# A hybrid decoder layer with 32 experts on one core: experts in 14 tiles instead of 16, a last tile by columns, two banks for head outputs, other places for S5 and the first loads

## The reference

```python
xn = rms_norm(h, mix_norm_g[l])
proj = jnp.einsum('bsd,de->bse', xn, w_in[l])
q_a, k_a, v_a, u_s5, q_h, f_h, i_h, g_h = jnp.split(proj, split_at, axis=-1)
attn_out = diff_attention(...)     # 6 heads, two softmaxes per head
s5_out = s5_mixer(...)             # 40 groups, 64 states, then z * sigmoid(z @ w_glu)
hgrn_out = hgrn2_mixer(...)        # 5 heads
mix = jnp.concatenate([attn_out, s5_out, hgrn_out], axis=-1)
h = h + jnp.einsum('bse,ed->bsd', mix, w_out[l]).astype(h.dtype)
hn = rms_norm(h, ffn_norm_g[l])
h = h + hier_moe(hn, ...)
return rms_norm(h, final_norm_g)
```

```python
expert_id = (g_idx[:, None] * EXPERTS_PER_GROUP + top_idx).reshape(-1)
order = jnp.argsort(expert_id)
xs = xt[order // TOP_K_IN_GROUP]
sizes = jnp.bincount(expert_id, length=N_EXPERTS).astype(jnp.int32)
h = jax.nn.silu(lax.ragged_dot(xs, w_gate, sizes)) * lax.ragged_dot(xs, w_up, sizes)
y = lax.ragged_dot(h, w_down, sizes) * gates_flat[order][:, None]
out = jnp.zeros_like(xt).at[order // TOP_K_IN_GROUP].add(y)
```

## Time and profile before

| | |
|---|---|
| median of 3 runs | 2043.24 us (2040.47 to 2047.9) |
| the profiled execution | 2040.63 us, its span 2038.7 us |
| mean granted clock of TensorE | 0.972 of full speed |
| busy: TensorE products / weight loads | 93% / 58% |
| VectorE / ScalarE / GpSimd | 40% / 12% / 9% |
| moved by DMA | 507.8 MB, 249 GB/s over the span |

### The profile page before, as it was taken

How to read it: one execution, slowest core, us unless ns; L and a number is a source line. 1 busy time by engine, 2 the same in 40 slices (tenths; PEclk the granted TensorE clock), 3 DMA queues, 4 the chain that set the end, 5 groups by cost and what they waited for, 6 DMA issues and landing times.

```text
span 2038.7 us, 32619 instructions
## 1 busy us (share of the span) xinstructions
PE 1899.3 (93%) x13695; PEld 1176.1 (58%) x13695; DVE 817.7 (40%) x1544; ACT 249.8 (12%) x551; POOL 189.5 (9%) x218
## 2 busy tenths in 40 slices
PE   5999999999999979999399998999999989999996
PEld 3888999789987869999233333332333323333332
DVE  6666585177456644333412121221222222122215
ACT  3012111100334331000200000000000000000002
POOL 1353332000000000000110000000000000000000
PEclk9999999999998989999699999999999999999998
DMA  5243333211221232121799999999999999999992
GB/s 210 85 146 92 90 97 85 94 63 42 71 74 58 68 141 82 65 82 42 304 422 424 423 425 422 408 424 416 411 423 404 423 412 410 423 403 423 391 378 104
DMA packets 74276, 507.81 MB, mean 249 GB/s; under 512 B 19184, under 2 KB 19332, under 8 KB 38160
## 3 DMA queue, kind: packets, MB, share of 16 engines
q1 hardware_dynamic: 56576, 485.60, 59.2%
q0 software_dynamic: 5728, 15.81, 2.3%
q10 hardware_dynamic: 11824, 4.17, 1.1%
HBM read 503.53 MB, written 12.99 MB: 253 GB/s over the span
## 4 chain that ended last, share of the span: by engine, by line
PE 80%; DMA 10%; DVE 4%; issue 3%; ACT 2%; SPq 0%; DVEq 0%; POOL 0%; POOLq 0%; ACTq 0%
PE psum L1151 21%; PE psum L850 19%; PE psum L853 15%; PE psum L1113 10%; DMA arena<-in_moe_w_gate 9%; PE psum L1170 7%; DVE arena L1453 2%; PE psum L1006 2%; PE psum L907 1%; PE psum L1126 1%; DMA arena<-hs_rows,arena 1%; DVE arena L1456 1%; PE psum L995 0%; DVE arena L2092 0%; PE psum L967 0%
## 5 line engine op out<-in xcount | busy, mean ns | idle before, releaser
L1151 PE MATMUL psum<-arena 128*32 128x512 f32 x4096 | 471.0, 607 | 37.9 <-issue 29.8
L1453 DVE TENSOR_TENSOR arena<-psum,arena 128x512 f32<-128x512 f32 x359 | 240.5, 687 | 443.4 <-PE psum L1113 423.9
L850 PE MATMUL psum<-arena 128*128 128x128 f32 x3584 | 412.9, 277 | 2.6 <-issue 2.6
L850 PEld LDWEIGHTS psum<-arena 128*128 128x128 f32 x3584 | 407.8, 194 | 9.8 <-issue 9.3
L1151 PEld LDWEIGHTS psum<-arena 128*32 128x32 f32 x4096 | 133.3, 112 | 367.3 <-issue 366.1
L853 PE MATMUL psum<-arena 128*128 128x256 f32 x1456 | 324.8, 382 | 1.9 <-DVE arena L533 1.3
L853 PEld LDWEIGHTS psum<-arena 128*128 128x128 f32 x1456 | 274.9, 191 | 40.8 <-issue 3.8
L1453 DVE TENSOR_TENSOR arena<-arena,psum 128x256 f32<-128x256 f32 (+2 forms) x174 | 76.5, 440 | 439.1 <-PE psum L850 211.3
L1113 PE MATMUL psum<-arena 128*128 128x512 f32 x512 | 236.0, 605 | 0.9 <-issue 0.9
L1170 PE MATMUL psum<-arena 128*32 128x512 f32 x2048 | 225.0, 597 | 2.6 <-DMA arena<-in_moe_w_down 2.1
L1453 DVE TENSOR_TENSOR arena<-arena 128x128 f32<-128x128 f32 (+17 forms) x446 | 177.8, 440 | 38.3 <-ACT arena L1230 30.1
(11 more groups left out here) (194 smaller groups left out, 950.1 us busy)
## 6 DMA issues: line engine op xcount, KB each, us to landing
arena<-in_moe_w_gate SPq DMA_DIRECT2D x64, 2048.0 KB, 23.9
arena<-in_moe_w_up SPq DMA_DIRECT2D x64, 2048.0 KB, 22.7
arena<-in_moe_w_down SPq DMA_DIRECT2D x64, 2048.0 KB, 22.7
arena<-in_w_in SPq DMA_DIRECT2D x86, 512.0 KB, 4.7
arena<-in_w_out SPq DMA_DIRECT2D x32, 512.0 KB, 4.6
arena<-in_x SPq DMA_DIRECT2D x8, 1024.0 KB, 8.8
hs_rows<-arena SPq DMA_DIRECT2D x4, 1024.0 KB, 5.1
out<-arena SPq DMA_DIRECT2D x4, 1024.0 KB, 4.0
```

Of the source, the lines that this page charges most:

```text
L850: last = mm(B(bank, [(1, P)], off=t * P), F(a + t * P, P), F(w + i * P, P), start=start and t == 0, stop=(i == KH - 1), skip_group_check=True)
L1151: last = mm(B(bank, [(1, FE)], 32 * g, 32), F(XT + c * CAP + 32 * g, 32), F(SLOT[slot] + (c % 8) * FE, FE), start=(c == 0), stop=(c == KD ...
L1453: return v.tensor_tensor(o, a, b, op)
```

## The change

1. **Tiles.** The 32 experts go into 14 tiles. `OWNERS` says which expert a group of 32 rows belongs to, `RANKS` which ranks (by size) a tile holds: the first tile has four experts with 32 rows each (ranks 16 to 19), eight tiles have 96 + 32 rows (rank i with rank 31 - i), four have 64 + 64 (8 + i with 15 - i), and the last again has four (20 to 23). TensorE's loop covers the eight; the four and both ends are written out. A table from the host gives each rank its rows; seven small operations of VectorE on the ranks go, two come ahead of `order_ready`.
2. **Loads.** SyncE reads four expert numbers and issues 24 halves for the first tile, then the loop of six iterations, then the last tile: 16 halves of gate and up, and its down weights by columns (four loads of columns 0 to 1023, four of 1024 to 1535, four of 1536 to 2047 that share the slots of the second four).
3. **Last tile.** The tile before it is combined as a whole first. TensorE spreads the final gain from one row over the partitions by four products. The down product and the combine go by quarters of 512 columns: quarters 0 and 1, their combines, quarter 2, its combine, quarter 3, its combine. Squares are summed by quarter on ScalarE, the gain is multiplied in by quarter on VectorE, and the scaling is shared: blocks 0 and 2 on VectorE, 1 and 3 on ScalarE.
4. **Attention's banks.** `ao` alternates between banks 3 and 2; the small steps have banks 0 and 1 plus spare ones. `attn_out` stands one unit later.
5. **S5.** For the last of the five blocks, `y5`, `yt` and `ge` stand at 9, 11 and 14 gaps instead of 10, 14 and 17.
6. **Start.** ScalarE takes a square root ahead of x. VectorE makes the first two weight sums ahead of the discretization; the sum `S4` of x (two operations) moves from the others to behind the first product, and TensorE waits for it at the seventh.
7. The overflow block gets semaphores of its own and is not overlapped with the tiles.

```diff
+CMIN = 32
+THREE_ONE, TWO_TWO, FOUR = (0, 0, 0, 1), (0, 0, 1, 1), (0, 1, 2, 3)
+OWNERS = [FOUR] + [THREE_ONE] * 8 + [TWO_TWO] * 4 + [FOUR]
+RANKS = [(16, 17, 18, 19)] + [(i, 31 - i) for i in range(8)] + [(8 + i, 15 - i) for i in range(4)] + [(20, 21, 22, 23)]
+NTILE = len(OWNERS)
+LAST = NTILE - 1
+A_END, B_END = 9, 13
...
+            y_at, yt_at, ge_at = (10, 14, 17) if more_ else (9, 11, 14)
...
-                          (6, [("sc", b, 4)]), (7, [("sc", b, 5)]), (10, [("y5", b, 0), ("y5", b, 1)]),
+                          (6, [("sc", b, 4)]), (7, [("sc", b, 5)]), (y_at, [("y5", b, 0), ("y5", b, 1)]),
...
             elif s[0] == "al":
-                small, ticking = [0, 1, 2], True
+                small, ticking = [0, 1], True
...
+            elif s[0] == "w4":
+                spare = [5, 6, 7]
             elif s[0] == "pe":
-                spare = []
+                spare = ([5, 6, 7], [6, 7], [], [])[s[1]]
...
-                bank = 3
+                bank = 3 - s[1] % 2
...
-            with sp.Fori(0, NPAIR // 2) as it:
+            four, parts = [expert(k) for k in range(4)], first_parts()
+            for j in range(FOUR_L):
+                part(four[j % 4], parts[j], j // 8, j // 4 % 2)
+            with sp.Fori(1, 1 + (B_END - 1) // 2) as it:
+                    two_, parts = [expert(it * 4 + 2 * k + i) for i in range(2)], pair_parts(it, k)
+                    for j in range(PAIR_L):
+                        part(two_[j % 2], parts[j], j // 4, j // 2 % 2)
...
+            sp.wait_ge(xT_full, 4 * B_END)
+            sp.dma_start(F(FG, D, 0, 1), DV(d["final_norm_g"], 0, [(D, 1), (1, D)])).then_inc(fg_in, 16)
+            four, parts = [expert(NE - 4 + k) for k in range(4)], last_parts()
+            for j in range(16):
+                part(four[j % 4], parts[j], j // 8, j // 4 % 2)
...
+            for k in range(4):
+                slot, n = parts[20 + k]
+                sp.wait_ge(slot_used[slot], n + 1)
+                sp.dma_start(V(SLOT[slot], [(512, FT2), (1, 512)]),
+                             down_columns(four[k], D // 2, 512)).then_inc(slot_in[slot], 16)
+            for k in range(4):
+                slot = parts[20 + k][0]
+                sp.dma_start(V(SLOT[slot] + D, [(512, FT2), (1, 512)]),
+                             down_columns(four[k], D // 2 + 512, 512)).then_inc(tail_in, 16)
             for t in range(TB):
-                sp.wait_ge(out_ready, t + 1)
+                sp.wait_ge((out_dve, out_act)[t % 2], 2 * (t // 2 + 1))
                 sp.dma_start(DV(out, t * P * D, [(D, P), (1, D)]), F(H0 + t * D, D)).then_inc(out_done, 16)
...
                     elif p == 0 and n == 2:
                         once(xsum_ready, 2)
+                    elif p == 0 and n == 6:
...
+                def y_part(q):
+                    here = parts[16 + 4 * (q // 2):20 + 4 * (q // 2)]
+                    if q == 3:
+                        pe.wait_ge(tail_in, 4 * 16)
+                    elif q != 1:
+                        for slot, before in here:
+                    for m in range(FT2):
+                        for g in range(4):
+                            at_ = m * (D // 2) + q * 512 if q < 2 else (q - 2) * D + m * 512
+                            last = mm(B(4 + q, [(1, 512)], 32 * g, 32), F(HTE + m * CAP + 32 * g, 32),
+                                      F(SLOT[here[g][0]] + at_, 512), start=(m == 0), stop=(m == FT2 - 1))
+                    last.then_inc(y_full, 1)
...
+                def combine_part(q):
+                    pe.wait_ge(y_act if q % 2 == 0 else y_dve, 2 * n + 2 + q // 2)
+                    if q == 0:
+                    for t in range(TB):
+                        if q:
+                            pe.wait_ge(comb_done, 16 * n + 4 * (q - 1) + t + 2)
+                        mm(B(t, [(1, 512)]), F(SEL + t * P, P), F(YSB + q * 512, 512), start=True,
+                           stop=True).then_inc(comb_full, 1)
+
+                y_part(0)
+                y_part(1)
+                combine_part(0)
+                combine_part(1)
+                y_part(2)
+                combine_part(2)
+                y_part(3)
+                combine_part(3)
...
-            for k in range(2):
-                pair_tile(k, k, 0, [pair_part(0, k, j) for j in range(12)], k > 0)
-            with pe.Fori(1, NPAIR // 2) as it:
+            expert_tile(0, 0, 0, first_parts(), FOUR, False)
+            with pe.Fori(1, 1 + (A_END - 1) // 2) as it:
                 for k in range(2):
-                    pair_tile(it * 2 + k, k, it, [pair_part(it, k, j) for j in range(12)])
+                    expert_tile(it * 2 - 1 + k, 1 - k, it - 1 + k, pair_parts(it, k), THREE_ONE)
+            for n in range(A_END, B_END):
+                expert_tile(n, n % 2, n // 2, pair_parts((n + 1) // 2, (n + 1) % 2), TWO_TWO, True, n + 1 < B_END)
...
+                pe.wait_ge(comb_done, 16 * LAST + 1)
+                with pe.Fori(0, NOV) as it:
+                    over_tile(it)
+                pe.wait_ge(o_added, NOV * 16 + 1)
+            turn(LAST, LAST % 2, LAST // 2, (0, 1, 2, 3), False, 16 * LAST)
+            pe.wait_ge(xT_free, 4 * LAST + 4)
+            last_tile(LAST, last_parts())
...
             act.wait_ge(eps_set, 1)
+            A(F(SM, 1), F(EPSC, 1), ACT.Sqrt)
             for t in range(TB):
...
+            y_copy(LAST, 2)
             for t in range(TB):
-                act.wait_ge(comb_done, 16 * (NPAIR - 1) + 4 * t + 5)
-                if t == 0:
-                    act.wait_ge(fg_in, 16)
-                deviation([F(H0 + t * D, D)], F(SLOT[7], D), SSQ + t, STD + t, D).then_inc(sum_std, 1)
+                square(t, 2)
...
+            def scaled(t):
+                act.wait_ge(h_rst, t + 2)
+                act.wait_ge(g_done, t // 2 + 1)
+                h = H0 + t * D
+                A(F(h, 1536), F(h, 1536), ACT.Copy, scale=F(RST + t, 1)).then_inc(out_act, 1)
+                A(F(h + 1536, 512), F(HG3 + t * 512, 512), ACT.Copy, scale=F(RST + t, 1)).then_inc(out_act, 1)
...
-                settle(tt(half(S2), half(S1), half(A11), SU))
-                last = tt(half(S4), half(A12), half(S2), SU)
+                last = tt(half(S2), half(S1), half(A11), SU)
...
+                        weight_sum(dve, v, 0, 0)
+                        weight_sum(dve, v, 0, 1)
                         disc_a()
                         disc_b()
...
+                elif s == ("pj", "u", 0):
+                    dve.wait_ge(xsum_ready, 1)
+                    tt(F(S4, KH * HB), F(A12, KH * HB), F(S2, KH * HB), SU).then_inc(xsum_ready, 1)
...
-                    if u >= 6 and u % TB == 2:
+                    if u > TB and u % TB == TB - 1:
                         attn_out(u // TB - 1)
...
+            dve.wait_ge(ranks_ready, 1)
+            two32 = [(NE, 2), (1, NE)]
+            settle(tt(V(ROP, two32, 0, NE), V(ROH, [(0, 2), (1, NE)], 0, NE), V(PLACE, two32, 0, NE), M))
+            settle(v.tensor_reduce(F(RMY, 2, 0, NE), V(ROP, two32, 0, NE), AX.X, AD))
...
+            for q in range(2):
+                for t in range(TB):
+                    add(t, q)
+            for q in range(2):
+                for t in range(TB):
+                    times_g(t, q)
...
+                add(t, 2)
+            for t in range(TB):
+                times_g(t, 2)
+            y_copy(3)
...
+            def scaled(t):
+                h = H0 + t * D
+                ts(F(h, 1536), F(h, 1536), F(RST + t, 1), None, M).then_inc(out_dve, 1)
+                v.scalar_tensor_tensor(F(h + 1536, 512), F(h + 1536, 512), F(RST + t, 1), F(FG + 1536, 512), M,
+                                       M).then_inc(out_dve, 1)
...
+            add(0, 3)
+            add(1, 3)
+            sum_of(0)
+            last_g(1)
+            add(2, 3)
+            inverse_of(0)
+            sum_of(1)
+            add(3, 3)
+            inverse_of(1)
+            scaled(0)
+            sum_of(2)
+            last_g(3)
+            inverse_of(2)
+            sum_of(3)
+            inverse_of(3)
+            scaled(2)
```

404 lines of the change are left out of this document (272 added, 132 removed).

## The result

| | before | changed |
|---|---|---|
| median of 4 runs | 2043.0 us | 1990.7 us (1987.7 to 1994.2) |
| ratio, 95% interval | | 0.9742 (0.9717 to 0.9766) |
| profiled execution, span | 2038.7 us | 1989.3 us |
| first weight load issued | 991.35 | 968.97 |
| last weight load landed | 1984 (a trickle until 1985.5) | 1962.9 |

The kernel is 2.6% faster. The forecast was 1985, inside a range of 1968 to 2008. Of the 49.4 us of the span, 22.4 come ahead of the first load and 28.3 behind the last landing; between the two they take the same within what can be told (993.9 for 992.7 up to 1984, or 994.2 up to 1985.5: in the old kernel the last packets of the weights trickle on at a DMA share of 0.08). The 28.3 and the 22.4 are the whole gain.

A forecast was written before the change was run, and what follows sets the result against it. TensorE was taken to bound the kernel up to 991 us, weight transfers after. First load at 968 plus 988 gave a last landing at 1956, plus 25 a span of 1981; forecast median 1985, range 1968 to 2008.

The forecast's parts named there:

- Start: Kernel start: early square root and moved weight sums remove table loads and TensorE waits, gaining 4.2 us (2.5 to 4.4).
- S5: Last S5 block: earlier scan output, transposed read and gelu remove TensorE's wait before the GLU, gaining 3.7 us (0 to 5).
- Attention: Attention heads: two output banks and later emptying remove TensorE's waits for ao and slow restarts, gaining 17 us (5 to 21).
- First loads: Before the first weight load: SyncE reads four expert numbers instead of two, costing 1.5 us (0.6 to 2.5).
- Expert stage: First load to last landing: same bytes at 421 then 423 GB/s, 976.3 us, plus 5, 4 and 2.4, making 988.
- the seam at the last tile: Before the last tile: slots come free after 39 us, eight loads ahead take 40; momentarily empty queue, +4 us (0 to 15).
- the short rows: Last down weights: loading by columns in rows of 4 and 2 KB slows transfers, +2.4 us, at worst +12.
- TensorE's lag: Pair tiles: TensorE falls behind the transfers by near 10 us at its peak, +5 us (2 to 14).
- The end: Behind the last landing T: work by column quarters, then norm and outputs, ends at T + 25 us (18 to 33).
- the starved queues: Rival, tiles of four: TensorE frees four slots at once and late, losing transfers, +12 us, 1997; chance 0.10.
- Small banks: Rival, attention: with two small banks the waits move from ao to the scores, the 17 us not gained, 2002; chance 0.08.
- The clock after waits: Rival, last tile and end: TensorE's clock stays at 1.2 GHz to the end, +24 us, 2009; chance 0.05.

The follow-up runs named there:

- the repeat: The changed kernel run again, unaltered, on one chip with later variants: median 1989.7 us, ratio 0.9745 to the kernel before.
- old_start: Changed kernel without the early square root and with the weight sums back in their old places: first load at 971.4, 4.6 us later.
- old_attention: Changed kernel with attention's old banks and old place of emptying the output bank: first load at 981.4, 14.6 us later.
- one_bank: Changed kernel with attention's old banks alone (output bank 3, three small banks), emptying kept late: first load at 998.2, 31.4 us later.
- old_place: Changed kernel with the output bank emptied one unit earlier, as before, new banks kept: first load at 987.2, ratio 0.9846 to the kernel before.
- late_gain: Changed kernel with the gain's spreading moved behind the first half of the last tile's gate product: median 1984.75 us, ratio 0.9715 to the kernel before.
- rows_last: Changed kernel with the last tile's down weights loaded by halves of rows, as before: ratio 0.9829 to the kernel before, span 2005.2 us.

## Why the prediction held, step by step

The span was forecast at 1981 and came at 1989.3 (1987.1 in the repeat), 8.3 us late: 1.0 at the first load, 5.9 in the expert stage, 1.4 at the end. The median is only 5.7 off since the forecast put it 4 us over the span, and it lay 1.4 over; that part is luck. So is the first load's hit: attention brought 4.5 less than the sum in the first profile, and the start, S5 and the first loads 0.9, 2.0 and 0.7 more. The terms:

- **Start**, 4.2 (2.5 to 4.4): 4.6 to 6.2. The pieces were the right ones and each came a little larger: in the first comparison 2.9 us are there at the first large product (2.6 in the sum), 1.4 and 0.7 for the two waits (1.3 and 0.6), so 5.1 where the bound was 4.4. The 6.2 in `old_start` hold 1.1 that come of TensorE's clock over the input products (last section).
- **S5**, 3.7 (0 to 5): 5.7 and 5.8 at the GLU, over the bound; 4.2 at the first load. The wait went, and so did TensorE's slow restart, which I had named and left out.
- **Attention**, 17 (5 to 21): 14.6 at the first load by `old_attention` (16.2 ahead of the clock's fall), 12.5 in the first profile; 17.0 until the last head. The size held, the reason only in part. I priced the second bank and the later emptying together, by TensorE's wait alone; by `one_bank` and `old_place` either by itself loses, and the place decides the sign of what the banks bring. The step that was weak is "ao of the next head waits for the bank that VectorE has yet to empty": true, but I did not ask what VectorE waits for, 4.1 us in each of five heads for ScalarE's root. That the last head gives 0.8 to 3.6 us back, TensorE waiting for the weights of the last units, was in no term.
- **First loads**, +1.5: behind the common products the lead shrank from 23.2 to 22.4, so 0.8 lost, inside 0.6 to 2.5.
- **First load** at 968: 969.0, and 967.0 in the repeat.
- **Expert stage**, 988 us from first load to last landing: 993.9. Two of its parts were measured: the seam at the last tile, +4 in the sum, is 5.1 by `late_gain`; the short rows, +2.4, are 2.2 by `rows_last`. The working of the seam held to a microsecond: from the landing of the pair's last half (1837.4) to the freed slots 40.2 us (39 in the sum), and eight landings in 39.2 us (40). But 39 against 40 makes no hole at all, and the +4 did not follow from it; what costs is that a load issued into an empty queue lands 7.3 us later, which the sum had not. What was undersized is the rest, 981.3 in the sum and 986.6 measured, although its 5 us for TensorE's lag, meant for a fall like the old kernel's, were not needed for one: the rate stayed at 421. That this is not 423 makes 3.0 us over 624; I had taken the rate of the earlier trace rows at its best stretch. Where the others lie no run shows; the last 22 us run at 348 GB/s, of which the short rows are a part, and DMA engines that run dry one after another would be the other.
- **The end**, T + 25 (18 to 33): T + 26.4. Every stage came within a microsecond: the first four pieces done at T - 5.8 (T - 6), the third quarter combined at T + 2.2 (T + 2), the last at T + 10.3 (T + 10). What is left behind it took 16.1 us, for 15.

Of the rivals, the starved queues came true in part: the hole is there, DMA share 0.52, under the 0.9 that I had named as the sign of being wrong, but it costs 5 us and not 12. Small banks do not choke attention as long as the emptying stands late. At the old place TensorE waits 15.5 us for the weights and 5.5 ahead of the scores (L1132; 1.9 in the changed kernel), and whether the missing small bank has a share in it is open. The clock after waits is real, 2.1 us at the end, not 24. The overflow block did not run.

## What to carry to other kernels

When TensorE waits for VectorE, look first at what VectorE waits for in its own queue; a second buffer without moving that wait only moves the stall, here from 14.6 us saved to 5.8 us lost (with one small bank less in both). Before a stage that frees buffers in groups, put everything that is not needed for the next free behind it: four small products moved were worth 5 us of transfers. Look there when each load is issued, not only when the queue runs dry: one issued 1.1 us after the last landing cost 3.5, since it needs 7.3 itself. At the end of a kernel bound by transfers, cut the last weights along the output, so that only one slice of product, combine and norm is left behind the last load: 20 us here, less 2 for the shorter rows.

## What the hardware showed that I had not expected

- The mean share of the DMA engines overstates a gap: 24 us at 0.52 cost 5 us, 25 us at 0.77 and 20 us at 0.89 none. Landings of loads are the better clock.
- Issuing a load can take long by itself. SyncE's issues of the last down weights, with rows of 4 KB (L695) and 2 KB (L700, L704), took up to 6.9 us, with four to six loads under way, where those of the last tile's up halves took 0.33 to 0.48. In `rows_last` the same weights in rows of 8 KB were issued, with three to six loads under way, in 0.37 to 0.42 us but for one of 1.73 (last row), so it goes with the short rows (ns, least, median and most):

```profile
L695 SPq DMA_DIRECT2D arena<-in_moe_w_down x4: 383/3218/6091, 1908.8 to 1915.9; - x4
...
L700 SPq DMA_DIRECT2D arena<-in_moe_w_down x4: 373/1519/6920, 1929.7 to 1938.2; - x4
...
L704 SPq DMA_DIRECT2D arena<-in_moe_w_down x4: 2413/2444/2513, 1940.8 to 1948.7; - x4
...
L641 SPq DMA_DIRECT2D arena<-in_moe_w_down x8: 372/400/1733, 1906.4 to 1929.0; - x8
```

- The same front issues its first load between 966.8 and 969.0. In one execution TensorE's first 32 products of 128 x 512 (S5's input) take 15.67 us and in another 13.97, and 28 products at the last head 5.17 or 3.36: its clock falls and rises at other moments relative to the same work (granted 0.50 from 730 to 734 in the first, 1.00 there in the second).
